# Five level masks of a triangular inverse go from VectorE's program to GpSimd's

## The chip, the cores and the metric

The kernel runs on one core of one Trainium2 chip, in float32. The metric is the device time of one execution in microseconds (us); lower is better. Five engines run their own programs and wait for each other with semaphores: TensorE (PE in the profile, its weight loads PEld), VectorE (DVE), ScalarE (ACT), GpSimd (POOL) and SyncE (SP, which issues most DMAs).

## The reference

Two transformer blocks on 512 tokens of width 1024 run one after the other. The first mixes by neighbourhood attention, by a bidirectional RWKV-7 recurrence and by memory attention, and then runs 16 experts; the second is a gMLP with banded attention and a product-key expert layer. The change lies in the recurrence, which has 6 heads of 64 and runs once in each direction d:

```python
def step(state, inp):
    r_t, w_t, k_t, v_t, a_t, b_t = inp
    sa = jnp.einsum('bhvk,bhk->bhv', state, a_t)
    state = state * w_t[:, :, None, :] + sa[..., None] * b_t[:, :, None, :] + v_t[..., None] * k_t[:, :, None, :]
    return state, jnp.einsum('bhvk,bhk->bhv', state, r_t)
```

The kernel doesn't step token by token. It takes 64 tokens as a chunk, in which the recurrence becomes products of small matrices and the inverse of a unit triangular 64x64 matrix for each head.

## The kernel before, in words

The recurrence runs in `pe_rw`, `dv_rw`, `ac_rw`, `po_rw` and `sp_rw`, one generator per engine, stepped in the same order by `steps_of`. For each direction d (0, 1) there is a `prep` stage (elementwise work over all 512 tokens), and then four rounds j = 0 to 3. A round is `matrix(d, j)`, which prepares two chunks (the inverses included), and `chunks(d, j - 1)`, which carries the state through the two chunks of the round before, woven into it. Between the steps `fill` places pieces of an unrelated projection (`wa_hi`, `wa_lo`, `h_hi`, `h_lo` in the profile), so that TensorE has work while it would wait. Nothing plans this at run time: every engine takes its instructions in the order in which they are written, and waits at each for the semaphores named there.

`matrix(d, j)` does this:

- TensorE multiplies, VectorE masks the products into `M4` (`m` in the profile; 4 instructions, L871). There are two `M4` buffers, for even and odd j.
- TensorE transposes operands into token layout (`tok`); ScalarE copies them out.
- VectorE makes level 0 of the inverse (L878 to L880, `inv_x`, called X1 in the code): two groups g of three heads, two tensor-tensor instructions each, both with two inputs in SBUF: `M4` by a mask in `cons`, then plus the unit matrix. The mark `z` follows each group, and TensorE waits for z of group g before its first product `t_ps` of that group (L750).
- Five doubling levels n = 1 to 5 follow. For level n TensorE needs `BT[n]` (`inv_b` in the profile), which is `M4` times the constant mask of that level, for all six heads in one 128x384 instruction with the mark `masked`. It multiplies it with `Tm` (`inv_t`), ScalarE copies the product to `inv_x`, TensorE multiplies again, ScalarE copies `inv_t` and VectorE adds to `TT` (`inv_tt`).

```python
    def level(eng, out, q, n, M4, name=None):
        eng.tt(out[:, q, :], M4[:, q, 0:64], row3(cons[:, C_LVL + 64 * n:C_LVL + 64 * n + 64], q.stop - q.start), MUL, name=name)
```

VectorE makes the mask of level 1 right after z, and that of level n + 1 at the start of level n (L881, L892). In `chunks`, VectorE's instructions on `u_a` and `inv_tt` read one operand from PSUM, those on `state` partly too. GpSimd's program in this stage (`po_rw`) has the `prep` instructions and one memset of the state; its `matrix` only keeps step (L909).

Every helper (`tt` is L115, `ts` L120, `cp` L130, `stt` L126, TensorE's `mm` L92) waits for the engine's own previous instruction to be complete before it issues the next (`own`).

Of the kernel before, what the change touches and what calls it, by code (L numbers as in the profile page):

```python
# [192 lines left out]
def block_program(nc, I, O):  # L193
# [9 lines left out]
    def A(name, off, *shape, dt=F32):  # L203
        assert D0 + off + int(np.prod(shape)) <= O_TAIL, (name, off, shape)
        return T(name, D0 + off, *shape, dt=dt)
# [18 lines left out]
    def row3(ap, n):  # L224
        return ap.rearrange("p (a b) -> p a b", a=1).to_broadcast([128, n, ap.shape[-1]])
# [26 lines left out]
    BT = [None] + [A(f"inv_b{i}", T1o + 2688 + 384 * i, 6, 64) for i in range(5)]  # L252
# [452 lines left out]
    M4_ALL = [(0, 0), (0, 1), (2, 0), (2, 1)]  # L705
    eye = cons[:, C_EYE:C_EYE + 64]

    def bufs(j):
        return M4s[j % 2], AToks[j % 2], Ats[j % 2], U0s[j % 2]

    def last_chunk(d, j):

        return [("y_ps", d, 2 * j - 3)] if j >= 2 else [("prep", d)]

    def heads(ap):
        return ap.rearrange("p (a b) -> p a b", b=64)
# [143 lines left out]
    def level(eng, out, q, n, M4, name=None):  # L860

        eng.tt(out[:, q, :], M4[:, q, 0:64], row3(cons[:, C_LVL + 64 * n:C_LVL + 64 * n + 64], q.stop - q.start), MUL, name=name)

    def dv_matrix(dv, turn, d, j):
        M4 = bufs(j)[0]
        for hs in M4H:
            w = 256 * len(hs)
            for e in range(2):
                b, use, _ = turn.next()
                dv.wait_ge(("m4_ps", d, j, hs[0], e), *last_chunk(d, j))  # L870
                dv.tt(M4[:, 2 * hs[0] + e:2 * hs[-1] + e + 1:2, :], PS[b][:, 0:w].rearrange("p (a b) -> p a b", b=256),  # L871
                      row3(cons[:, C_M4:C_M4 + 256], len(hs)), MUL, name=use)
                dv.mark(("m4", d, j, hs[0], e))
            yield
        for _ in range(4):
            turn.next()
        yield
        for g, q in enumerate(HG):  # L878
            level(dv, X1, q, 0, M4)
            dv.tt(X1[:, q, :], X1[:, q, :], row3(eye, 3), ADD, name=("z", d, j, g))  # L880
        level(dv, BT[1], slice(0, 6), 1, M4, name=("masked", d, j, 1))  # L881
        if j:
            dv.wait_ge(("u0_ps", d, j - 1))
        for g, q in enumerate(HG):
            b, use, _ = turn.next()
            dv.wait_ge(("t_ps", d, j, 0, g))
            dv.cp(TT[:, q, :], heads(PS[b][:, 0:192]), name=use)
            dv.mark(("tt", d, j, 0, g))
            yield
        for n in range(1, 6):  # L890
            if n < 5:
                level(dv, BT[n + 1], slice(0, 6), n + 1, M4, name=("masked", d, j, n + 1))  # L892
            for g in range(2):
                turn.next()
                yield
            for g, q in enumerate(HG):
                b, use, _ = turn.next()
                dv.wait_ge(("t_ps", d, j, n, g))
                dv.tt(TT[:, q, :], TT[:, q, :], heads(PS[b][:, 0:192]), ADD, name=use)
                dv.mark(("tt", d, j, n, g))  # L900
                yield
        turn.next()
        yield
        turn.next(), turn.next()
        yield
        turn.next()
        yield

    def po_matrix(po, d, j):  # L909
        for i in range(28):  # L910
            yield

    def pe_chunks(pe, turn, d, j):
# [127 lines left out]
    def dv_rw(dv):  # L1041
        fill = Filler(dv_filler(dv))
        turn = Turn("pb", PB)
        for d in range(2):
            steps_of(d, lambda d: dv_prep(dv, turn, d), lambda d, j: dv_matrix(dv, turn, d, j),
                     lambda d, j: dv_chunks(dv, turn, d, j), fill)
        fill.rest()
# [9 lines left out]
    def po_rw(po):  # L1057
        for d in range(2):
            steps_of(d, lambda d: po_prep(po, d), lambda d, j: po_matrix(po, d, j),
                     lambda d, j: po_chunks(po, d, j), lambda n: None)  # L1060
# [1615 lines left out]
```

## Time and profile before

| | |
|---|---|
| time, median of 3 runs | 3373.69 us (3373.23 to 3374.45) |
| time of the profiled execution | 3373.69 us |
| its span | 3371.5 us |
| PE, busy in the span | 2694.9 us (80%) |
| DVE | 1635.3 us (49%) |
| ACT | 997.9 us (30%) |
| POOL | 662.3 us (20%) |
| direction 0, rounds and last chunks | 186 to 316 us |
| direction 1, rounds and last chunks | 416 to 550 us |

The span is counted from the first to the last instruction; the 2.2 us between it and the time of the execution lie around it. Busy times are sums over one execution, so an engine's share tells of the average and not of one stage; the times of single rows are read from the span's start.

### The profile page before, as it was taken

How to read it: one execution, taken by the hardware profiler on the slowest of the kernel's cores; microseconds unless marked ns; L12 is line 12 of the kernel's file. 1: busy time of each engine (PE TensorE's matmuls, PEld its weight loads, DVE VectorE, ACT ScalarE, POOL GpSimd, SP SyncE). 2: the span in 40 equal slices, each digit the busy share in tenths (PEclk: the TensorE clock that was granted, in tenths of full speed). 3: DMA queues.
4: the chain of work that ended last, by engine and by line, in shares of the span. 5: the costliest groups of instructions: out<-in, count | busy, mean ns of one | idle time of the engine just before them, and what ended most of it. 6: DMA issues, size and time to landing. Idle time of an engine off the chain costs nothing.

```text
span 3371.5 us, 43915 instructions
## 1 busy us (share of the span) xinstructions
PE 2694.9 (80%) x17232; PEld 1379.7 (41%) x17232; DVE 1635.3 (49%) x3438; ACT 997.9 (30%) x2395; POOL 662.3 (20%) x563
## 2 busy tenths in 40 slices
PE   8799897785999999999997887787768655555555
PEld 6577675383333333333337663343324311111111
DVE  4756755754100100100107357667676677776664
ACT  2233143410000000000003335477554334433332
POOL 0401300000000000000000023333443444444442
PEclk9899898997999999999998798897979877777777
DMA  3221212127999999999993289999999999999997
GB/s 146 78 71 63 93 48 107 71 93 314 420 420 420 419 420 420 419 420 420 420 393 128 79 338 401 419 394 383 381 416 420 384 420 420 420 420 420 420 420 325
DMA packets 156190, 1068.86 MB, mean 317 GB/s; under 512 B 17360, under 2 KB 19280, under 8 KB 30544
## 3 DMA queue, kind: packets, MB, share of 16 engines
q0 software_dynamic: 75408, 543.20, 39.2%
q1 hardware_dynamic: 80576, 522.87, 38.3%
q8 instruction: 135, 2.21, 0.3%
q14 instruction: 71, 0.58, 0.0%
HBM read 1052.63 MB, written 13.37 MB: 316 GB/s over the span
## 4 chain that ended last, share of the span: by engine, by line
PE 54%; DMA 25%; DVE 13%; ACT 5%; issue 2%; POOL 1%; DVEq 0%; ACTq 0%; SPq 0%; POOLq 0%
PE ps L92 52%; DMA gb<-in_peer_uv,eidx 25%; DVE gb L146 2%; PE ps L97 2%; ACT L168 1%; ACT dots L168 1%; ACT diag L168 1%; POOL gb L86 1%; DVE wa_lo L115 1%; DVE expert_act L115 1%; DVE prob L146 0%; DVE wa_hi L130 0%; DVE rw_r L126 0%; DVE prob L120 0%; ACT prob L168 0%
## 5 line engine op out<-in xcount | busy, mean ns | idle before, releaser
L92 PE MATMUL ps<-gb,diag 64*64 64x512 f32 x4096 | 659.3, 767 | 441.9 <-ACT diag L168 425.7
L146 DVE CUSTOM_DVE_ANT_0 gb<-gb,xn 128x1024 f32<-128x1024 f32 x512 | 626.7, 1224 | 365.8 <-DMA gb<-in_peer_uv,eidx 365.8
L86 POOL DMA_INDIRECT gb<-in_peer_uv,eidx x512 | 566.6, 1107 | 987.0 <-PE ps L92 731.7
L92 PEld LDWEIGHTS ps<-gb,diag 64*64 64x64 f32 x4096 | 150.4, 158 | 880.2 <-ACT diag L168 783.5
L92 PE MATMUL ps<-ga,xt 128*64 128x512 f32 x1120 | 331.5, 602 | 2.5 <-DVE xt L120 2.5
L115 DVE TENSOR_TENSOR expert_act<-expert_act,ps 128x512 f32<-128x512 f32 x32 | 22.0, 687 | 541.6 <-PE ps L92 541.1
L168 ACT ACTIVATE dots<-dots 128x1 f32<-128x1 f32 (+1 forms) x374 | 75.9, 203 | 638.4 <-DVE dots L146 632.9
L115 DVE TENSOR_TENSOR x<-x,ps 128x512 f32<-128x512 f32 (+1 forms) x96 | 61.4, 643 | 367.1 <-PE ps L92 366.4
L168 ACT ACTIVATE diag<-cons,dots 128x128 f32<-128x128 f32 x512 | 205.5, 401 | 42.0 <-ACT dots L168 0.4
L92 PEld LDWEIGHTS ps<-ga,xt 128*64 128x64 f32 x1120 | 118.8, 137 | 187.9 <-issue 180.4
L92 PE MATMUL ps<-h_hi,wa_hi 128*128 128x512 f32 x368 | 158.3, 430 | 33.7 <-DVE wa_lo L115 32.9
L168 ACT ACT_TABLE_LOAD x139 | 178.3, 1283 | 9.4 <-PEq L2669 0.7
L92 PE MATMUL ps<-ga,expert_act_t 128*64 128x512 f32 x544 | 169.4, 602 | 0.0
L92 PE MATMUL ps<-gr,xt 128*64 128x512 f32 x528 | 163.6, 598 | 0.0
L168 ACT ACTIVATE dots<-dots,soft 128x1 f32<-128x1 f32 x512 | 150.8, 294 | 16.6
L92 PE MATMUL ps<-h_lo,wa_hi 128*128 128x512 f32 x368 | 148.3, 403 | 0.0
L92 PE MATMUL ps<-h_hi,wa_lo 128*128 128x512 f32 x368 | 148.2, 403 | 0.0
L92 PE MATMUL ps<-ring,xt 128*64 128x512 f32 x400 | 128.1, 598 | 0.0
L168 ACT ACTIVATE expert_act<-ps 128x512 f32<-128x512 f32 x32 | 19.1, 597 | 352.0 <-PE ps L92 351.5
L92 PE MATMUL ps<-f_t,ring 128*128 128x256 f32 x512 | 120.8, 397 | 2.2 <-DVE f_t L120 1.2
L86 POOL DMA_INDIRECT xe<-h_scratch,expert_idx x8 | 7.6, 949 | 583.8 <-PE ps L97 552.9
L92 PEld LDWEIGHTS ps<-f_t,ring 128*128 128x128 f32 x512 | 101.0, 200 | 28.5 <-issue 13.8
(331 smaller groups left out, 3946.6 us busy)
## 6 DMA issues: line engine op xcount, KB each, us to landing
ring<-in_wt SPq DMA_DIRECT2D x77, 1024.0 KB, 5.7
ga<-in_eg SPq DMA_DIRECT2D x70, 1024.0 KB, 26.2
ga<-in_eu SPq DMA_DIRECT2D x70, 1024.0 KB, 27.4
ga<-in_ed SPq DMA_DIRECT2D x68, 1024.0 KB, 27.7
gr<-in_eu SPq DMA_DIRECT2D x37, 1024.0 KB, 26.9
gr<-in_ed SPq DMA_DIRECT2D x34, 1024.0 KB, 27.4
ring<-in_eg SPq DMA_DIRECT2D x29, 1024.0 KB, 26.5
gr<-in_eg SPq DMA_DIRECT2D x29, 1024.0 KB, 27.0
```

Of the source, the lines that this page charges most:

```text
L86: self.e.indirect_dma_start(out, None, table, bass.IndirectOffsetOnAxis(ap=idx, axis=0)).then_inc(s, 16)
L92: i = self.e.matmul(out, l, r, start=st, stop=sp, skip_group_check=True)
L97: i = self.e.transpose(out, in_, ident[0:in_.shape[0], 0:in_.shape[0]])
L115: self.done(self.e.tensor_tensor(o, a, b, op), name)
L146: self.done(self.e.tensor_tensor_reduce(out=o, in0=a, in1=b, scale=scale, scalar=start, op0=o0, op1=o1, accum_out=acc), name)
L168: self.done(self.e.activation(o, a, f, **k), name)
```

## The change

The five masks of the levels 1 to 5 are no longer in VectorE's `matrix`, but in GpSimd's. Level 0 stays on VectorE. GpSimd waits for all four marks of `M4` of the round; from the second round of a direction on it waits, at level n, also for TensorE's last product that read `BT[n]` in the round before. It then issues the five masks one after the other, right at the top of the round. The constants, the buffers, the products and every number computed are the same.

```diff
@@ dv_matrix
         for g, q in enumerate(HG):
             level(dv, X1, q, 0, M4)
             dv.tt(X1[:, q, :], X1[:, q, :], row3(eye, 3), ADD, name=("z", d, j, g))
-        level(dv, BT[1], slice(0, 6), 1, M4, name=("masked", d, j, 1))
...
         for n in range(1, 6):
-            if n < 5:
-                level(dv, BT[n + 1], slice(0, 6), n + 1, M4, name=("masked", d, j, n + 1))
             for g in range(2):
@@ po_matrix
-        for i in range(28):
+        M4 = bufs(j)[0]
+        yield
+        yield
+        for n in range(1, 6):
+            po.wait_ge(*[("m4", d, j, *i) for i in M4_ALL])
+            if j:
+                po.wait_ge(("x_ps", d, j - 1, n, 1))
+            level(po, BT[n], slice(0, 6), n, M4, name=("masked", d, j, n))
+        for i in range(26):
             yield
```

On VectorE, in the second round of direction 0 (`m_1` is the odd `M4`, `inv_b_91` to `inv_b_95` are `BT[1]` to `BT[5]`), this changes:

```order
 L115 TENSOR_TENSOR inv_x<-m_1_87,cons 128x192
 L115 TENSOR_TENSOR inv_x<-inv_x,cons 128x192
-L115 TENSOR_TENSOR inv_b_91<-m_1_87,cons 128x384
 L130 COPY inv_tt<-ps 128x192 x2
-L115 TENSOR_TENSOR inv_b_92<-m_1_87,cons 128x384
 L115 TENSOR_TENSOR state_100<-ps,state_99 128x192
 L115 TENSOR_TENSOR state_100<-state_100,decay_end 128x192
 L115 TENSOR_TENSOR inv_tt<-inv_tt,ps 128x192 x2
-L115 TENSOR_TENSOR inv_b_93<-m_1_87,cons 128x384
```

What stood between the instructions on `inv_tt`, `state` and `y_sum` is gone; nothing else on VectorE has moved.

On GpSimd, at the start of the rounds of direction 0, the masks now stand in a row behind the memset of the state, with nothing of another kind between them:

```order
 L142 MEMSET state_99 128x192
+L115 TENSOR_TENSOR inv_b_91<-m_0_86,cons 128x384
+L115 TENSOR_TENSOR inv_b_92<-m_0_86,cons 128x384
+L115 TENSOR_TENSOR inv_b_93<-m_0_86,cons 128x384
+L115 TENSOR_TENSOR inv_b_94<-m_0_86,cons 128x384
+L115 TENSOR_TENSOR inv_b_95<-m_0_86,cons 128x384
+L115 TENSOR_TENSOR inv_b_91<-m_1_87,cons 128x384
```

The first five belong to j = 0, and the sixth is the first of j = 1; 20 stand so in each direction. On TensorE the order is the same and only the semaphore is another, at the first product of each level (`dve_rw0` is VectorE's counter in direction 0, `pool_rw` GpSimd's):

```order
-L92 MATMUL ps<-inv_t,inv_b_91 64x64 [waits act_rw0,dve_rw0]
+L92 MATMUL ps<-inv_t,inv_b_91 64x64 [waits act_rw0,pool_rw]
 L92 MATMUL ps<-inv_t,inv_b_91 64x64 x5
```

## Rows read from the trace of the kernel before

**Rows 1.** Busy time by stretch: start:end, length, busy us of each engine, clock, DMA.

```profile
186.00:316.00 130.00, 122.97 (x2825) 94.86 (x2824) 71.08 (x160) 44.53 (x118) 0.00 (x0) 1.00 0.12 39
```

**Rows 2.** Chain that ended last, direction 0: start us, us, what.

```profile
218.03 0.36 DVE u_a L115
...
219.97 0.37 DVE inv_x L115
...
220.38 0.58 PE ps L92 x24
220.98 7.76 PE ps L92 x199
...
287.18 0.57 DVE inv_b L115
```

**Rows 3.** Waits, 186 to 550 us: who <- for whom, us in total, times, longest.

```profile
PEld ps L92 <- DVE inv_x L115: 11.8, 13, 3.5
...
PEld ps L92 <- DVE inv_b L115: 1.6, 7, 0.5
...
PE ps L92 <- DVE inv_tt L115: 4.0, 7, 1.1
```

**Rows 4.** The tile inv_b: duration ns min/median/max, first and last start, form.

```profile
L115 DVE TENSOR_TENSOR inv_b<-m,cons x40: 557/558/560, 193.2 to 526.6; 128x384 f32<-128x384 f32 x40
```

**Rows 5.** Timeline of DVE, d = 0, j = 1: start us, us, what, idle before.

```profile
214.34 2.55 DVE L115 TENSOR_TENSOR m<-ps,cons 128x512 f32<-128x512 f32 x4 [3.37 <-PE ps L92]
...
218.79 0.36 DVE L115 TENSOR_TENSOR inv_x<-m,cons 128x192 f32<-128x192 f32 x1
...
219.97 0.36 DVE L115 TENSOR_TENSOR inv_x<-inv_x,cons 128x192 f32<-128x192 f32 x1
220.36 0.56 DVE L115 TENSOR_TENSOR inv_b<-m,cons 128x384 f32<-128x384 f32 x1
```

**Rows 6.** The timeline of DVE, d = 0, j = 0.

```profile
189.02 2.54 DVE L115 TENSOR_TENSOR m<-ps,cons 128x512 f32<-128x512 f32 x4 [2.88 <-PE ps L92]
191.60 0.36 DVE L115 TENSOR_TENSOR inv_x<-m,cons 128x192 f32<-128x192 f32 x1
...
192.78 0.36 DVE L115 TENSOR_TENSOR inv_x<-inv_x,cons 128x192 f32<-128x192 f32 x1
```

**Rows 7.** The timeline of DVE, d = 1, j = 3.

```profile
508.04 0.95 DVE L115 TENSOR_TENSOR m<-ps,cons 128x256 f32<-128x256 f32 x2 [0.47 <-PE ps L92]
...
511.66 1.54 DVE L120 TENSOR_SCALAR mem_x<-mem_x,small 128x1024 f32<-128x1024 f32 x2
...
514.41 0.36 DVE L115 TENSOR_TENSOR inv_x<-inv_x,cons 128x192 f32<-128x192 f32 x1
```

**Rows 8.** Timelines of DVE and POOL where both worked, in order of time.

```profile
80.40 0.69 DVE L115 TENSOR_TENSOR rw_t<-p_w 128x512 f32<-128x512 f32 x1 [4.12 <-ACT lat_g L168]
80.45 3.25 POOL L115 TENSOR_TENSOR rw_p<-p_v 128x1536 f32<-128x1536 f32 x1 [56.07 <-ACT lat_g L168]
...
117.89 3.78 POOL L115 TENSOR_TENSOR rw_k<-rw_k,rw_p 128x1536 f32<-128x1536 f32 x1
118.39 4.37 DVE L115 TENSOR_TENSOR wa_lo<-ring,wa_hi 128x1024 fp32r<-128x1024 f32 x1
121.81 4.27 POOL L115 TENSOR_TENSOR rw_p<-rw_r,rw_k 128x1536 f32<-128x1536 f32 x1
...
153.68 1.23 DVE L115 TENSOR_TENSOR wa_lo<-ring,wa_hi 128x1024 fp32r<-128x1024 f32 x1
...
351.56 3.42 POOL L115 TENSOR_TENSOR rw_p<-rw_r,rw_k 128x1536 f32<-128x1536 f32 x1 [0.63 <-DVE rw_r L126]
...
1776.62 2.92 DVE L120 TENSOR_SCALAR xn_mix<-x,small 128x1024 f32<-128x1024 f32 x1
1776.64 2.34 POOL L115 TENSOR_TENSOR w_s<-w_s,cons 128x1024 f32<-128x1024 f32 x1 [411.19 <-DMA w_s<-in_wsT]
```

**Rows 9.** Timeline of the DMA queue of SP, the first expert tiles.

```profile
769.41 4.07 SPq L80 DMA_DIRECT2D ga<-in_eg  x8
```

## The prediction, made before the changed kernel was run

> **What bounds the kernel now.** I read the busy shares by stretch first. In the rounds of direction 0, from 186 to 316 us, TensorE is busy for 122.97 of 130 us at the full granted clock (1.00, the 2.4 GHz level), VectorE for 71.08 and GpSimd for nothing [rows 1]. So the stage belongs to TensorE, GpSimd is free, and taking work off VectorE can pay only where TensorE stands and waits for it.
>
> The chain that ended last says where that is. In round j = 1 it goes through VectorE's `u_a`, then through the `inv_x` that ends group 1 of level 0, then at 220.38 into TensorE and stays there for 0.58 and 7.76 us on end [rows 2]. The other rounds with j > 0 have the same piece. The reader is to see two things: TensorE takes up the inverse the moment `inv_x` is ready, and behind it lies solid TensorE work, so that a delay of `inv_x` is not made good. The masks, `inv_b`, stand on the chain once in direction 0, with 0.57 us at 287.18 [rows 2], and not in direction 1.
>
> The waits agree: from 186 to 550 us TensorE's weight loads stood 11.8 us for `inv_x`, in 13 places, and 1.6 us for `inv_b`, in 7 [rows 3]. Level 0 is the sore spot and the masks are nearly free.
>
> **What is removed.** 2 directions x 4 rounds x 5 masks are 40 instructions of 0.558 us [rows 4], 22.3 us of VectorE time. On the path they are worth the 1.6 us of waits and the 0.57 us link: 2.2 us. Could VectorE's other work come sooner and release TensorE elsewhere? It waited 4.0 us for `inv_tt` [rows 3]; at those places `inv_tt` mostly stands behind `y_sum` or `wa_hi` and `wa_lo`, which stay. I give it nothing in the sum and keep a gain of 2.2 + 4.0 = 6.2 us as the far end.
>
> **What is added: are the masks late for TensorE?** GpSimd has no 128x384 instruction before. Its tensor-tensor rows are 2.34 us for 1024 elements, 3.25 and 3.42 us for 1536 [rows 8]: 2.29, 2.12 and 2.23 ns an element, so 0.81 to 0.88 us for 384 if there is no fixed part. A line through 2.34 and 3.25 has 0.52 us fixed and 1.78 ns an element, and gives 1.20 us. I take 0.9 us, next to the 1024 row, the shortest there is, and keep 0.8 and 1.2. Between two of them I put 0.1 us for the hand-over: its next tensor-tensor began at 121.81, when the one before had ended at 117.89 + 3.78 = 121.67. `M4` is complete at 214.34 + 2.55 = 216.89 [rows 5]; GpSimd starts at about 216.98, has mask 1 at 217.9 and alone would have all five at 221.9. TensorE takes mask 1 at 220.98 [rows 2] and mask 5 a dozen us later. The waits for `x_ps` of the round before are long fulfilled. So no mask is late, even at 1.2 us, and what is queued behind them on GpSimd is only the next round's masks. The wait on `inv_b` goes.
>
> **What the masks do to VectorE.** This is the term that decides. The rows with both engines at work show VectorE standing still. `wa_lo` takes 1.23 us when GpSimd is idle; beside GpSimd's tensor-tensor of 117.89 to 121.67 it was issued at 118.39 and ended at 122.76, 1.09 us after GpSimd's end: 4.37 us [rows 8]. It has two inputs in SBUF, as each of the four `inv_x` instructions has. A tensor-scalar over 1024 elements, 0.77 us where two take 1.54 [rows 7], took 2.92 us and ended 0.56 us after GpSimd's tensor-tensor, which had begun 0.02 us later [rows 8]. And the next GpSimd instruction behind `wa_lo` took 4.27 us where its like of direction 1 took 3.42 [rows 8]: it in turn let VectorE through first. So they alternate, one whole instruction each. A blocked VectorE instruction ends its own duration less about 0.14 to 0.2 us after GpSimd's; for 0.36 us I put 0.25.
>
> The five masks now run just when level 0 is made. For j = 1, with 0.9 us each:
> - masks 1 and 2 run from 216.98 to 218.88; the two `u_a` instructions run beside them;
> - the first `inv_x`, issued at 218.79 [rows 5], is held to 218.88 and ends at 219.13; mask 3 to 220.03, the second ends at 220.28; mask 4 to 221.18, the third at 221.43; mask 5 to 222.33, the fourth at 222.58.
> Before, the fourth ended at 219.97 + 0.36 = 220.33 [rows 5]. The delay is 2.25 us (1.99 at 0.8 us a mask, 3.75 at 1.2), and TensorE, which waited at 220.38, waits it out in full.
>
> Whether `u_a` is held too, no row shows: it reads one operand from PSUM and only one from SBUF, and both VectorE instructions of [rows 8] that were held are of another kind. Held by no mask it gives 2.25, held by a mask each 3.0 us. I take the first, since none of the held rows has its operands. The Trainium skill (SBUF — State Buffer, "Who interferes with whom") says that a VectorE instruction with at most one SBUF input, outside the two-port modes, does not contend with GpSimd. By that rule the sum stands, and by its opposite it would be about 4 us higher.
>
> For j = 0 there is no `u_a`. `M4` ends at 191.56, the first `inv_x` starts at 191.60 [rows 6], ahead of GpSimd, and ends at 191.96; three pairs of 1.15 us follow, and the fourth `inv_x` ends at 195.41 instead of 192.78 + 0.36 = 193.14: 2.27 us. (An instruction of VectorE that was 0.05 us ahead did run its usual 0.69 us [rows 8].) For d = 1, j = 3, `M4` ends at 508.99 and two `mem_x` of 0.76 us lie before `inv_x` [rows 7]; they are of the held kind as well. Mask 3 ends at 511.98, the first `mem_x` at 512.54, mask 4 at 513.44, the second at 514.0, mask 5 at 514.9, and by then `inv_x` is free: the fourth ends near 516.3 instead of 514.77, 1.5 us.
>
> **The sum.** Five rounds with j > 0 at 2.25 make 11.25, two rounds j = 0 at 2.27 make 4.5, the last 1.5: 17.3 us. Less 2.2 us: +15.1 us. At 0.8 us a mask it is 15.0 - 2.2 = +12.8, at 1.2 us 28.2 - 2.2 = +26.0. Behind the stage nothing takes it back: the expert tiles are asked for at 769.41, when TensorE's last product of the merge is done [rows 9], so this stream shifts with TensorE. The profiled execution took 3373.69 us, 2.2 more than its span, and is itself the median of the runs shown: 3373.7 + 15.1 = 3388.8, say 3389 us.
>
> **Rivals.** About 0.2%, 6.7 us, is what can be told from no change here.
> - The two engines don't hold each other at such short instructions. For it: VectorE's 80.40 row ran its normal 0.69 us while GpSimd's tensor-tensor of 3.25 us had begun at 80.45 [rows 8]. Against it: it was first, and every later one was held. The mechanism would then be the plain one: level 0 as before, the mask of level 1 ready 3 us early, `inv_b` out of the chain. It decides if a mask holds VectorE for less than about 0.1 us each. 3373.7 - 2.2 = 3371.5 us, and with the far end 3367.5: not slower. Chance 0.10, and another 0.03 that something of VectorE's relief that I don't see makes it faster by more than 6.7 us.
> - The engines hold each other, but for part of GpSimd's row only, since its spans are rough. At half the hold the sum is 17.3 / 2 - 2.2 = +6.5: 3380 us. Chance 0.09, half of it on each side of the bound.
> - GpSimd doesn't let VectorE in between its masks. VectorE then waits for the whole burst to 221.9 and makes `inv_x` after it, ending near 223.3: 3.0 us a round, 22 us in all: 3396 us. Against it speaks the 4.27 us row. Chance 0.06.
> - The masks are late because a short GpSimd instruction costs about as much as a long one. At 3.25 us each, mask 5 comes at 233.7 before any hold, and every `inv_x` of a round waits over 3 us: 8 rounds x 10 us or more, 3450 us. The 2.34 us row speaks against it. Chance 0.02.
>
> My forecast, the alternation with masks of 0.8 to 1.2 us, keeps 0.70, with 3386 to 3400 us as its own range. Slower than 0.2%: 0.70 + 0.06 + 0.02 + 0.05 = 0.83. Within: 0.10 + 0.04 = 0.14. Faster: 0.03. The range leaves out the first rival and the last, and runs from 3379 to 3401 us.
>
> **What the profile after would show.** Right: GpSimd has 40 instructions of 0.9 to 1.2 us, in bursts of five; the 32 `inv_x` instructions of VectorE take well over 0.36 us, near 0.9 in most; `u_a` still takes 0.36 each; TensorE's waits for `inv_x` grow from 11.8 us by some 15, those for `inv_b` vanish; the expert tiles are asked for some 15 us later. The order of `inv_x`, mask, `inv_x`, mask in the timeline shows the alternation. Wrong: `inv_x` at 0.36 us throughout, or TensorE waiting for masks of GpSimd, or a late start of the masks.

## The result: 3404 us, slower by twice what was forecast

| | median us | runs | ratio to before, 95% interval |
|---|---|---|---|
| before | 3373.46 (3372.51 to 3374.45) | 4 | |
| changed kernel | 3403.93 (3398.0 to 3409.49) | 4 | 1.0088 [1.007, 1.0105] |
| changed kernel again, with the experiments | 3402.12 (3400.14 to 3402.85) | 5 | 1.0082 [1.0068, 1.0096] |

Forecast were 3389 us with a range to 3401: the direction was right, the size half. Over all 24 executions of the changed kernel on record it ranged from 3394.80 to 3416.50 us, with a median of 3401.86. The profiled execution took 3399.32 us with a span of 3397.5, 26.0 more than before.

The masks and level 0 in the profile after (the tile views, durations min/median/max):

```profile
L115 POOL TENSOR_TENSOR inv_b<-m,cons x40: 991/995/1257, 191.4 to 537.2; 128x384 f32<-128x384 f32 x40
...
L115 DVE TENSOR_TENSOR inv_x<-m,cons x16: 357/1037/1117, 191.2 to 539.1; 128x192 f32<-128x192 f32 x16
L115 DVE TENSOR_TENSOR inv_x<-inv_x,cons x16: 359/1099/1103, 191.5 to 539.5; 128x192 f32<-128x192 f32 x16
```

A mask takes 0.995 us instead of 0.558 [rows 4], and level 0, untouched in the code, went from 0.36 to a median of 1.04 and 1.10 us an instruction (27 of the 32 were held). VectorE's timeline in round j = 1 of direction 0, which answers to [rows 5]:

```profile
220.58 0.73 DVE L115 TENSOR_TENSOR u_a<-ps,u 64x192 f32<-64x192 f32 x2 [1.15 <-PE ps L92]
221.35 0.76 DVE L115 TENSOR_TENSOR inv_x<-m,cons 128x192 f32<-128x192 f32 x1
222.14 1.10 DVE L115 TENSOR_TENSOR inv_x<-inv_x,cons 128x192 f32<-128x192 f32 x1
223.28 1.10 DVE L115 TENSOR_TENSOR inv_x<-m,cons 128x192 f32<-128x192 f32 x1
224.41 1.10 DVE L115 TENSOR_TENSOR inv_x<-inv_x,cons 128x192 f32<-128x192 f32 x1
```

and GpSimd's beside it:

```profile
219.75 0.99 POOL L115 TENSOR_TENSOR inv_b<-m,cons 128x384 f32<-128x384 f32 x1 [23.06 <-PE ps L97]
220.89 1.00 POOL L115 TENSOR_TENSOR inv_b<-m,cons 128x384 f32<-128x384 f32 x1
222.03 0.99 POOL L115 TENSOR_TENSOR inv_b<-m,cons 128x384 f32<-128x384 f32 x1
```

In this round the masks start every 1.14 us, and each `inv_x` ends 0.2 us after one of them ends: 220.89 + 1.00 = 221.89, and 221.35 + 0.76 = 222.11. The two `u_a` instructions, one input in SBUF, ran over the end of mask 1 and into mask 2 unharmed, in 0.73 us. The chain of waits has the same piece, and with it the answer to [rows 2]:

```profile
224.41 1.11 DVE inv_x L115
225.52 0.04 issue
225.57 9.60 PE ps L92 x224
```

The waits from 186 to 550 us, against [rows 3]:

```profile
PEld ps L92 <- DVE inv_x L115: 31.0, 15, 5.5
...
PE ps L92 <- DVE inv_tt L115: 2.9, 4, 1.1
```

TensorE's weight loads wait 19.2 us more for `inv_x`; the 1.6 us for `inv_b` are gone, as forecast. What I had not put in the sum stands in the stretches. First the one over direction 0, with the columns of [rows 1]:

```profile
186.00:322.00 136.00, 119.66 (x2707) 92.43 (x2706) 65.89 (x130) 43.93 (x117) 19.92 (x20) 0.94 0.11 36
```

and then shorter ones, of TensorE alone (start:end, length, busy, clock, DMA share, GB/s):

```profile
220.00:226.00 6.00, 2.43 (x56) 0.97 0.12 44
226.00:230.00 4.00, 4.00 (x86) 0.62 0.02 4
254.00:258.00 4.00, 1.45 (x27) 0.79 0.00 0
258.00:262.00 4.00, 3.34 (x44) 0.50 0.01 4
290.00:294.00 4.00, 0.69 (x28) 0.99 0.00 0
294.00:298.00 4.00, 4.00 (x74) 0.59 0.01 4
```

The granted clock over direction 0 was 1.00 [rows 1] and is 0.94. In each of these rounds, once TensorE has stood behind the held level 0, its clock is at 0.50, which is 1.2 GHz, for 3 to 7 us (most of the stretches above are wider and show a mean), and only then 2.4 GHz again.

**Where the 26 us are.** The length of a direction, direction 0 from VectorE's first `m` to GpSimd's first instruction of direction 1, and direction 1 from the first `m` to the last `y_sum`, and of the rounds in direction 0 from one first `m` to the next, all read from the timelines of the profiled executions:

| us | round 0 | round 1 | round 2 | direction 0 | direction 1 |
|---|---|---|---|---|---|
| before | 25.32 | 29.21 | 30.53 | 127.72 | 129.42 |
| changed | 28.32 | 33.08 | 34.88 | 142.71 | 140.31 |
| e6_warm_fitted | 27.04 | 31.67 | 33.00 | 136.75 | 137.46 |
| e3_delay_full | 29.01 | 33.16 | 34.92 | 143.73 | 145.38 |
| e3_delay_half | 26.35 | 30.39 | 32.77 | 135.87 | 139.77 |
| e1_after_level0 | 25.66 | 31.21 | 32.50 | 132.07 | 131.65 |
| e2_first_on_dve | 25.30 | 29.20 | 30.54 | 127.25 | 130.94 |
| e7_split_masks | 25.64 | 28.97 | 30.31 | 127.58 | 129.32 |
| e5_warm_last_only | 25.33 | 29.20 | 30.53 | 127.70 | 128.30 |
| e9_level0_early | 25.33 | 28.30 | 29.50 | 124.74 | 125.35 |
| e10_early_masks_pool | 25.66 | 28.25 | 29.42 | 124.44 | 125.38 |

The two directions grew by 15.0 and 10.9 us, 25.9 together, against 26.0 in the whole profiled execution. Nearly all of the loss lies in the changed stage, but that the two numbers agree so well is partly luck. The expert tiles are asked for at 797.40 instead of 769.41 [rows 9], 28.0 us later. Of that, 3.3 us arose between the end of direction 1 and the tiles, where no instruction has changed, and 1.2 us were gained ahead of the two directions and between them; behind the tiles 2.0 us came back. The stretch from the end of direction 1 to the tiles, before and after, TensorE alone:

```profile
551.32:769.41 218.09, 175.21 (x934) 0.90 0.27 104
575.97:797.40 221.43, 180.56 (x934) 0.88 0.26 103
```

The same 934 products took 5.4 us more at a lower clock. In the other profiled executions this stretch took 219.0 to 221.4 us, so the kernel before has the shortest of them.

### The profile page after: what moved, and what is told of

Read it like the earlier page. It is cut to its first block, busy times and chain, and to the rows that moved or that the text cites. A ratio compares the mean times of both kernels' runs of the same rounds, so it can differ in the third digit from the quotient of the medians.

```text
span 3397.5 us, 43961 instructions
## 1 busy us (share of the span) xinstructions
PE 2700.4 (79%) x17232; PEld 1384.2 (41%) x17232; DVE 1632.4 (48%) x3398; ACT 997.8 (29%) x2395; POOL 699.3 (21%) x603
## 4 chain that ended last, share of the span: by engine, by line
PE 52%; DMA 27%; DVE 13%; ACT 6%; issue 2%; POOL 1%; DVEq 0%; SPq 0%; ACTq 0%; POOLq 0%
PE ps L92 50%; DMA gb<-in_peer_uv,eidx 25%; DVE gb L146 2%; PE ps L97 2%; ACT L168 1%; ACT dots L168 1%; DMA ga<-in_ed 1%; DVE inv_x L115 1%; POOL gb L86 1%; ACT diag L168 1%; DVE expert_act L115 1%; DVE wa_lo L115 1%; ACT prob L168 0%; DVE rw_r L126 0%; DVE wa_hi L130 0%
```

## The experiments

Each ratio is to the kernel before on the same chip, whose medians there were 3371.48 us (beside e1, e2, e3_delay_full and e4), 3372.33 (beside e3_delay_half, e5, e6 and e7) and 3373.47 (beside the changed kernel again, e8, e9 and e10). With 21 to 23 runs each that kernel ranged from 3368 to 3379 us, so differences under 3 us are read from the stage lengths above. In the experiments that held level 0 or delayed it, the medians lie 3 to 6 us further from the kernel before than the two directions together, except for e3_delay_half; where in the kernel that part lies is open.

**The changed kernel again.**

> The changed kernel once more, on the chip of the three beside it: 26 to 32 us above the kernel before, about 3400 to 3403 us, with the granted clock at 0.50 for some us in most rounds behind a held level 0. This fixes how much of it e6_warm_fitted took away on the same scale.

3402.12 us, with stage lengths of 142.69 and 140.31 us: the loss repeats.

**e1_after_level0: GpSimd waits for level 0.**

```diff
-            po.wait_ge(*[("m4", d, j, *i) for i in M4_ALL])
+            po.wait_ge(("z", d, j, 1))
```

> The changed kernel, but GpSimd starts its five masks only when VectorE has finished level 0 (the mark z of group 1) instead of when M4 is complete. Nothing else is moved. Theory A (the loss comes from the masks holding VectorE's level-0 instructions, and from the clock that falls while TensorE waits for them): the inv_x instructions of VectorE are back at 0.36 us, TensorE's waits for inv_x fall from 31.0 us back to about 12, its granted clock is 1.00 in all rounds but the last; mask 1 now ends about 1.1 us after level 0 where VectorE made it in 0.56, so each round loses at most 0.5 us, and the state instruction with two SBUF inputs may be held once a round: 3373 to 3382 us. Theory B (masks on GpSimd are slow or late in themselves, whatever they hold): no better than the changed kernel, 3400 us or more, with TensorE waiting for inv_b.

3379.38 us, ratio 1.0022 [1.0012, 1.0031]: 22 of some 30 us are gone with one wait moved. Level 0 is back at 0.36 us. What stays is the late mask 1:

```profile
PEld ps L92 <- DVE inv_x L115: 12.1, 14, 3.5
PEld ps L92 <- POOL inv_b L115: 5.1, 9, 0.6
```

The clock, which I expected at 1.00, still fell twice in direction 0, in rounds 1 and 2, after a wait of only 0.6 us for `inv_b` that came on top of the usual ones. The cost per round is up to 2.0 us (31.21 against 29.21), not 0.5.

**e2_first_on_dve: mask 1 back on VectorE, four on GpSimd behind it.**

```diff
+        level(dv, BT[1], slice(0, 6), 1, M4, name=("masked", d, j, 1))
...
-        for n in range(1, 6):
-            po.wait_ge(*[("m4", d, j, *i) for i in M4_ALL])
+        for n in range(2, 6):
+            po.wait_ge(("masked", d, j, 1))
```

> The changed kernel with the mask of level 1 back on VectorE, right after level 0, and GpSimd's four other masks waiting for it. Theory A: no hold of level 0 and no late first mask: within 3 us of the kernel before, 3371 to 3376 us; TensorE waits for inv_x about 12 us. If GpSimd's burst holds the state instruction of VectorE (two inputs in SBUF) by up to 1 us a round, 3376 to 3380. Theory B: more than 3385.

3376.32 us, 1.001 [1.0001, 1.0019]. Direction 0 is 0.5 us shorter than before, direction 1 is 1.5 longer, since the clock fell once more there, at 538 us. Four masks a round on GpSimd cost next to nothing when they don't meet level 0, and relieving VectorE of them gains almost nothing.

**e3_delay_full and e3_delay_half: a late level 0 without GpSimd, in the kernel before.**

```diff
         for g, q in enumerate(HG):
+            for _ in range(3 if g == 0 else 4):
+                level(dv, X1, q, 0, M4)
             level(dv, X1, q, 0, M4)
```

(1 and 2 in the half.)

> The kernel before, all masks on VectorE and GpSimd idle, with level 0 made slower by repeating its first, idempotent instruction: 3 more times in group 0 and 4 more in group 1, 0.39 us each, so that the mark z comes 1.2 us (group 0) and 2.7 us (group 1) later, as in the changed kernel. Theory A (a late level 0 is all there is, and TensorE's clock falls behind it): the same loss as the changed kernel or a little more, since the masks still load VectorE: 3400 to 3412 us, granted clock 0.50 for about 4 us in most rounds, and runs that spread by 10 us or so as those of the changed kernel do. Theory C (the clock and the spread belong to GpSimd's work): 8 x 2.7 = 21.6 us at most, 3395 us, clock 1.00, spread 2 us.

3408.54 us, 1.011 [1.0095, 1.0125], and the clock falls as in the changed kernel, here in round 1:

```profile
226.00:230.00 4.00, 2.79 (x39) 0.65 0.02 4
```

Rounds 1 and 2 are as long as those of the changed kernel to 0.1 us. Direction 1 is 5.1 us longer than there: the delay of 2.7 us is the same in every round, the first and the last included, and the clock fell in all eight rounds, the first of direction 1 included. GpSimd does nothing in the rounds here. So the fall of the clock needs no work on GpSimd; it follows from the delay. The spread that I expected (10 us) didn't come: 3405.41 to 3409.25.

> As e3_delay_full, but 1 more instruction in group 0 and 2 more in group 1 (0.39 and 1.17 us later). Theory A with a clock that falls or not by how long TensorE waits: the delay itself costs at most 8 x 1.17 = 9.4 us; if the clock stays at 1.00 in most rounds, 3377 to 3382 us, which is less than half of the 37 us of the full delay (1.17/2.7 of it would be 16 us, 3387.5). If the loss simply goes with the delay, 3387 us.

3389.33 us, 1.0055 [1.0041, 1.0069], outside what theory A gave and near the 3387 of a loss that simply goes with the delay. Round 1 kept its clock and lost 1.18 us, the delay alone; round 2, with the same delay, lost 2.24 and showed this:

```profile
248.00:252.00 4.00, 2.44 (x42) 1.00 0.27 113
252.00:256.00 4.00, 3.45 (x54) 0.57 0.01 4
```

The clock fell in more rounds than I had assumed, in two of direction 0 and in all but the first of direction 1, so the loss came out near the proportional one though rounds 1 and 2 differ by 1.1 us at the same delay. Of the five rounds with a fall, four had kept their clock in the kernel before; for them a delay of 1.2 us was enough.

**e4_warm and e6_warm_fitted: TensorE kept at work while level 0 is held, in the changed kernel.** The results of these dummy products are overwritten.

```diff
             b, use, before = turn.next()
-            pe.wait_ge(("z", d, j, g), *before)
+            pe.wait_ge(*before)
+            for _ in range(((1, 5) if j == 0 else (22, 4) if (d, j) == (1, 3) else (7, 5))[g]):
+                pe.mm(PS[b], h2[0][:, 0, 0:128], h2[0][:, 0, :])
+            pe.wait_ge(("z", d, j, g))
```

(e4_warm has 8 and 6 everywhere.)

> The changed kernel with dummy products on TensorE (128x512, about 0.23 us each, results overwritten) where it waits for level 0: 8 before group 0 and 6 before group 1 of every round. Nothing waits for them but TensorE's own order. Theory A with the clock as the second half of the loss: the clock stays at 1.00 in seven rounds (perhaps not in the last, whose wait of 5.5 us is longer than 8 products), the holds on inv_x stay, and the time falls to 3388 to 3394 us with a small spread. If the clock is not a cause: 3400 us or more, as the changed kernel.

3399.14 us, 1.0074 [1.0059, 1.0089]. The clock was 1.00 through all rounds of direction 0, yet the time missed my 3388 to 3394: the dummies were too many. Round 0 took 28.55 us, 0.2 more than in the changed kernel, whose clock had dropped there, and direction 1 took 141.53 us, 1.2 more; in its last round the clock fell all the same.

> As e4_warm, with the dummy products fitted to the waits of the changed kernel's trace: 1 and 5 in the rounds j = 0, 7 and 5 in those with j > 0, 22 and 4 in the last round of direction 1, so that TensorE isn't kept past the time at which level 0 is ready. In e4_warm the clock was 1.00 all through direction 0, but the dummies cost up to 1.5 us in a round j = 0. Theory A: clock 1.00 in all eight rounds, rounds with j > 0 in direction 0 about 2.5 us longer than before (31.7 and 33.0 us), j = 0 about 26.8: 3385 to 3392 us. If the clock isn't a cause: 3399 us or more, as e4_warm.

3394.94 us, 1.0067 [1.0054, 1.0081]. The clock is 1.00 in all eight rounds, for instance

```profile
218.00:224.00 6.00, 5.73 (x66) 1.00 0.12 44
224.00:230.00 6.00, 5.66 (x131) 1.00 0.01 3
252.00:258.00 6.00, 5.33 (x83) 1.00 0.06 23
258.00:264.00 6.00, 6.00 (x183) 1.00 0.01 3
```

while VectorE is held as before (`inv_x` at a median of 1.04 us). More work, and the directions are 6.0 and 2.9 us shorter than in the changed kernel. Since nothing was taken away, that is the clock's part, and a lower bound, as the dummies cost something themselves. In the whole time the gain is less clear: it is 22.6 us above the kernel before on its chip, where the changed kernel again is 28.7 above, and the two intervals of the ratio overlap. The stage lengths carry the reading; the changed kernel's two profiled executions agree in them to 0.02 us. The median is 3 us above the range I gave.

**e5_warm_last_only: the same dummies in the one round in which the clock of the kernel before fell.** Its edit is the above in the kernel before, with 12 dummies in group 0 of (d, j) = (1, 3).

> The kernel before, all masks on VectorE, with 12 dummy products only in the last round of direction 1, where TensorE stands 3.5 us for level 0 behind the two mem_x instructions and its clock is 0.50 to 0.86 from about 512 to 520 us. Theory A: that clock stays at 1.00 and direction 1 is 2 to 3 us shorter, 3368.5 to 3370 us against 3371.5 for the kernel before. If the clock has nothing to do with the time: no shorter, or longer.

3373.81 us, 1.0008 [0.9999, 1.0017]: no gain that can be told, and not the 2 to 3 us that I expected. The clock was mended, though. Before:

```profile
512.00:516.00 4.00, 1.96 (x58) 0.61 0.00 0
516.00:520.00 4.00, 4.00 (x96) 0.54 0.01 4
```

and with the dummies:

```profile
512.00:516.00 4.00, 3.30 (x61) 1.00 0.00 0
516.00:520.00 4.00, 4.00 (x141) 1.00 0.02 4
```

Direction 1 became 1.1 us shorter, which the whole time can't show.

**e7_split_masks and e8_split_warm: five masks on GpSimd, placed apart.** The edit is in the changed kernel; e8_split_warm adds the 12 dummies of e5_warm_last_only.

```diff
+            if n == 1:
                 po.wait_ge(*[("m4", d, j, *i) for i in M4_ALL])
+            elif n < 4:
+                po.wait_ge(("z", d, j, 1))
+            else:
+                po.wait_ge(("x_ps", d, j, 2, 1))
```

> All masks on GpSimd, but apart: mask 1 as soon as M4 is complete (as in the changed kernel), masks 2 and 3 after level 0, masks 4 and 5 after TensorE's product x_ps of level 2. Theory A: for j > 0 mask 1 runs while VectorE waits for u_ps and holds nothing; for j = 0 it holds the second inv_x by about 0.7 us, most of it where TensorE is still busy. Masks 2 to 5 fall where VectorE has nothing with two SBUF inputs. TensorE neither waits for inv_b nor longer for inv_x: rounds as before or 0.1 to 0.6 us shorter, 3369 to 3373 us. Theory B (masks on GpSimd cost by themselves): above 3376 us as in e1_after_level0 or e2_first_on_dve.

3374.04 us, 1.0006 [0.9997, 1.0015], 1 us above the range that theory A gave and below the 3376 of theory B; rounds 1 and 2 each 0.2 us shorter than before, round 0 0.3 longer, where mask 1 holds one `inv_x` (1.06 us). All five masks on GpSimd are thus free if placed well, and gain nothing that the time shows.

> e7_split_masks with 12 dummy products in the last round of direction 1 only, where its clock was 0.50 to 0.93 from 510 to 520 us. Theory A: direction 1 about 1 us shorter than in e7_split_masks (129.3 us from the first m to the last y_sum), as e5_warm_last_only was 1.1 us shorter there than the kernel before; in the whole time no difference that can be told: 3370 to 3375 us.

3377.07 us, 1.0009 [1.0, 1.0018], 2 us above the range I gave. Direction 1 took 128.21 us, 1.1 less than in e7_split_masks, and its clock stayed at 1.00; the time is again no measure of it.

**e9_level0_early and e10_early_masks_pool: level 0 moved ahead, the masks on VectorE or on GpSimd.** e9 is this edit in the kernel before; e10 is the same in the changed kernel, with GpSimd waiting for level 0 as in e1_after_level0.

```diff
         for _ in range(4):
             turn.next()
-        yield
         for g, q in enumerate(HG):
             level(dv, X1, q, 0, M4)
             dv.tt(X1[:, q, :], X1[:, q, :], row3(eye, 3), ADD, name=("z", d, j, g))
+        yield
```

> The kernel before, masks on VectorE, with one thing moved: VectorE makes level 0 right behind M4, ahead of the u_a instructions of the round before and of whatever filler stands there, where it now waits for TensorE's u_ps for 1.15 us. If level 0 is the sore spot that the waits show (11.8 us of TensorE's weight loads), it is ready 1.9 us earlier in the rounds with j > 0, and in the last round of direction 1 also ahead of the two mem_x. Then u_a is at most 0.4 us later. Theory A: TensorE's waits for inv_x fall from 11.8 to about 2 us, the clock stays at 1.00 in the last round, and the stage is 6 to 12 us shorter: 3360 to 3366 us. If TensorE's waits are only shifted to the next link (u_a, inv_t): 3369 us or more.

3364.35 us, 0.9974 [0.9962, 0.9986]: faster than both kernels. VectorE makes level 0 in the time in which it waited for `u_ps`:

```profile
214.82 2.55 DVE L115 TENSOR_TENSOR m<-ps,cons 128x512 f32<-128x512 f32 x4 [3.38 <-PE ps L92]
217.40 0.36 DVE L115 TENSOR_TENSOR inv_x<-m,cons 128x192 f32<-128x192 f32 x1
...
218.58 0.36 DVE L115 TENSOR_TENSOR inv_x<-inv_x,cons 128x192 f32<-128x192 f32 x1
219.07 0.73 DVE L115 TENSOR_TENSOR u_a<-ps,u 64x192 f32<-64x192 f32 x2
219.84 0.56 DVE L115 TENSOR_TENSOR inv_b<-m,cons 128x384 f32<-128x384 f32 x1
```

and the waits of TensorE become

```profile
PEld ps L92 <- DVE inv_b L115: 4.9, 8, 2.2
PEld ps L92 <- DVE inv_x L115: 2.6, 7, 0.4
```

The directions are 3.0 and 4.1 us shorter. A part of the wait for `inv_x` has gone over to `inv_b`, which now stands behind `u_a`. One thing that I expected didn't come: in the last round of direction 1 the clock fell here too, though for half as long as before:

```profile
510.00:514.00 4.00, 4.00 (x104) 0.58 0.02 4
```

> e9_level0_early with all five masks on GpSimd, started when level 0 is done. Theory A: level 0 is not held; the burst of about 5 us starts at M4 plus 1.6 us, next to u_a (one input in SBUF, not held: 0.36 us each), mask 1 is ready as TensorE comes for it, and at most the state instruction is held. Same as e9_level0_early within 4 us, 3360 to 3370 us. Theory B: 8 us or more above e9_level0_early.

3367.07 us, 0.9983 [0.9974, 0.9992], with stage lengths equal to those of e9_level0_early within 0.3 us. Here the wait on VectorE's mask is gone, TensorE waits 2.4 us for GpSimd's instead, and so the masks on GpSimd again gain nothing that can be measured, though level 0 is free of them. Other VectorE instructions are not: in the last round the two `mem_x` take 2.16 us there instead of 1.54 [rows 7].

## Why the prediction was right and wrong

**Right:** what bounds the stage, and which term decides. Where TensorE waited for level 0 already, it passes a further delay on nearly in full (1.17 us made round 1 of e3_delay_half 1.18 us longer); the masks are never late for it; VectorE's instructions with two SBUF inputs are held by GpSimd's, one whole instruction each; `u_a` is not held. e1_after_level0 shows the hold to be the cause by its absence. The relief of VectorE is worth next to nothing: e2_first_on_dve and e7_split_masks have it without the hold, and don't beat the kernel before; in e7 the two directions are 0.2 us shorter together (0.2 in each of rounds 1 and 2, with 0.3 lost in round 0), not 2.2. I had also taken the waits for `inv_tt` from the row of the products (4.0 us) and those for `inv_x` and `inv_b` from the rows of the weight loads. The weight loads' own row for `inv_tt` is larger:

```profile
PEld ps L92 <- DVE inv_tt L115: 11.1, 26, 1.2
```

It fell to 3.3 us in the changed kernel and to 4.6 in e7_split_masks, and e7 gained nothing by it.

**The size of the hold** was near. A mask takes 0.995 us and the next starts 1.14 us after it, where I took 0.9 and 1.0. No mask was lengthened by an `inv_x`, as I had read from the 4.27 us row; `inv_x` fits in at the end of one mask. Beside the `mem_x` instructions of the last round two masks did take 1.26 us. From the first `m` to the end of the fourth `inv_x` it is 224.41 + 1.10 - 216.89 = 8.62 us in round j = 1, against 220.33 - 214.34 = 5.99 before: 2.63 us, forecast 2.25; in j = 2 of direction 0 and j = 1 of direction 1 it is the same, and in the two others of this kind (j = 3 of direction 0, j = 2 of direction 1) 3.0. In j = 0 it is 2.06 us, forecast 2.27, and in the last round 2.0, forecast 1.5. Together the delays are 20.0 us, where I had 17.3. With the clock kept up the two directions grew by 9.0 and 8.0 us, 17.1 together (e6_warm_fitted); my sum was 15.1. That these are so close is partly luck: the delays were longer than I had them, but where TensorE had still been busy at that moment, not all of one reached it: of the 2.06 us in the first round of direction 1, 1.4.

**The step that failed** is the sentence that TensorE "waits it out in full", taken as the whole price. I read the clock as 1.00 in the view by stretch and left it out of the sum. But standing still has a price of its own: after it, the clock was 0.50 for some 3.5 us in five of the eight rounds and for some 7 us in two. That is 31 us at half speed, which by my estimate could cost at most half of it, 15 us. Rounds 1 and 2 of direction 0 cost 3.87 and 4.35 us more than before; with the clock kept at 1.00 they cost 2.46 and 2.47 more, so 1.4 and 1.9 us are the clock. Over the stage it is at least 8.8 us, 25.9 less 17.1. In the prediction's terms: 15.1 us forecast, 2.0 more for delays and relief, 8.8 for the clock that stood in the sum at nothing, which makes 25.9 in the stage; the medians differ by 28.7 and 30.5 us, and the 3 to 5 us beyond the stage are not explained. The first round of direction 1 is a control that the changed kernel has in itself: level 0 held as in the first round of direction 0, the clock stayed,

```profile
436.00:446.00 10.00, 7.77 (x154) 1.00 0.41 161
```

and the round was 1.4 us longer, not 3.0 as its like in direction 0.

The trace before had the sign: in the last round of direction 1, behind a wait of 3.5 us for `inv_x` [rows 3], its clock was 0.61 and 0.54 over 8 us (the fence at e5_warm_last_only). I used that longest wait as a number and didn't ask what the clock did behind it.

The Trainium skill (SBUF — State Buffer, "Summary: rules for kernel authors") says that when VectorE's instruction has two SBUF inputs and GpSimd's reads SBUF, the second one to issue is blocked until the first finishes. The trace agrees: all 27 `inv_x` issued during a mask ended 0.2 us after that mask, and the first `inv_x` of both rounds j = 0, issued 0.2 us ahead of mask 1, took 0.36 us.

**Open:** why the clock falls in one round and not in the next with the same delay (e3_delay_half, rounds 1 and 2) was not settled. Nor was the time outside the stage: the medians of the changed kernel are 3 to 5 us further from the kernel before than its stage, and no run isolates where they lie; from the expert tiles to the end alone the profiled executions differ by up to 6 us.

## What to carry to other kernels

Before work goes from VectorE to an idle GpSimd, look at what VectorE does in that very moment: an instruction with two SBUF inputs waits for GpSimd's to end, so four instructions of 0.36 us on a critical path turned into four of up to 1.1 us. Letting GpSimd start behind them brought back 22 of the 30 us. Where TensorE bounds a stage, price a new wait twice, once by its length and once by the clock behind it, and look in the trace before for places where a wait of that length already is. And where the waits name one instruction as the sore spot, move that one: level 0 ahead of `u_a` gained 9 us (7 in the stage), and moving 22 us of other work off its engine gained nothing.

## What the runs showed of the hardware

- GpSimd's 128x384 tensor-tensor takes 0.99 us and repeats every 1.14 us (1.08 in the rounds j = 0, which have one semaphore to wait for fewer); the line through its two longer sizes had given 1.20, the proportion 0.88.
- A hold lasts to the end of the mask: no `inv_x` of round j = 1 that was issued during a mask got through before the mask was over, though the second had 0.9 us of it left, and the masks there became no longer by it (a burst of five takes 5.56 us in e1_after_level0, where it meets no level 0, and 5.55 in the changed kernel).
- TensorE's clock fell behind waits for level 0 that came to 4.1 us in round j = 1 (1.5 before, where it stayed). No single stop of its products there was longer than 1.9 us, and in round 1 of e1_after_level0, where the clock fell too, none was longer than 0.7 us. A row of dummy products of 0.23 us each was enough to keep it at 2.4 GHz: extra work made the stage 8.8 us shorter.
